# Turning the blocks of x behind the slabs, and who makes the low parts of slabs 1 and 3, at the start of a 1144-slab kernel

## What is computed

```
x = x + 0.5 * _swiglu(_rmsnorm(x, ffn1_norm[l]), ffn1_w_gu[l], ffn1_w_down[l])

def _rmsnorm(x, g):
    xf = x.astype(jnp.float32)
    y = xf * lax.rsqrt(jnp.mean(xf * xf, axis=-1, keepdims=True) + RMS_EPS)
    return (y * g.astype(jnp.float32)).astype(x.dtype)

def _swiglu(h, w_gu, w_down):
    gate, up = jnp.split(h @ w_gu, 2, axis=-1)
    return (jax.nn.silu(gate) * up) @ w_down
```

## Time and profile before

| | before |
|---|---|
| median of 3 runs | 3111.97 us |
| profiled execution | 3111.83 us, its span 3110.0 us |
| TensorE busy | 3072.0 us, 99% of the span |
| VectorE, ScalarE, GpSimd busy | 63%, 47%, 41% |
| DMA engines, mean | 212 GB/s read |
| granted TensorE clock, mean | 0.997 |

### The profile page before, as it was taken

How to read it: one execution, slowest core, us unless ns; L and a number is a source line. 1 busy time by engine, 2 the same in 40 slices (tenths; PEclk the granted TensorE clock), 3 DMA queues, 4 the chain that set the end, 5 groups by cost and what they waited for, 6 DMA issues and landing times.

```text
span 3110.0 us, 46519 instructions
## 1 busy us (share of the span) xinstructions
PE 3072.0 (99%) x19062; PEld 2714.9 (87%) x19062; DVE 1945.6 (63%) x2394; ACT 1446.4 (47%) x1877; POOL 1279.5 (41%) x621
## 2 busy tenths in 40 slices
PE   8999999999999999999999999999999999999998
PEld 7888888888999999998888888888899998899986
DVE  5777577773323446773466767676479864589764
ACT  5444444344567545544544444344444454444444
POOL 4444444444566554584444444444710004510013
PEclk9999999999999999999999999999999999999999
DMA  7878778785776555565787778787776545765454
GB/s 224 287 247 278 263 263 273 250 284 175 220 172 183 156 166 147 149 173 194 237 270 256 274 254 274 245 290 244 188 197 194 159 136 197 165 196 180 152 164 167
DMA packets 491774, 664.11 MB, mean 214 GB/s; under 512 B 74137, under 2 KB 278665, under 8 KB 491305
## 3 DMA queue, kind: packets, MB, share of 16 engines
q1 hardware_dynamic: 486072, 655.72, 67.1%
q0 software_dynamic: 4448, 3.64, 0.5%
q10 hardware_dynamic: 1040, 1.78, 0.2%
HBM read 656.82 MB, written 2.10 MB: 212 GB/s over the span
## 4 chain that ended last, share of the span: by engine, by line
PE 95%; DMA 1%; DVE 1%; ACT 1%; issue 1%; POOL 0%; SPq 0%; ACTq 0%; DVEq 0%
PE ps L891 36%; PE ps L819 22%; PE ps L896 18%; PE ps L825 11%; PE ps L809 2%; DMA stage<-in_w_in 1%; PE ps L850 1%; PE ps L1352 1%; PE ps L1137 1%; PE ps L1118 1%; POOL narrow_split_slabs L769 0%; PE ps L950 0%; PE ps L1045 0%; DMA x_res<-in_x 0%; PE ps L1175 0%
## 5 line engine op out<-in xcount | busy, mean ns | idle before, releaser
L769 POOL TENSOR_TENSOR split_slabs<-stage,split_slabs 128x1024 fp32r<-128x1024 f32 x296 | 751.0, 2538 | 1363.6 <-ACT split_slabs L1407 1363.6
L1407 ACT ACTIVATE split_slabs<-stage 128x1024 fp32r<-128x1024 f32 x592 | 627.1, 1061 | 903.9 <-PE ps L896 675.0
L891 PE MATMUL ps<-split_slabs,h_split 128*128 128x512 f32 x3312 | 827.1, 392 | 0.9 <-ACT split_slabs L1407 0.9
L1407 ACT ACTIVATE narrow_split_slabs<-stage 128x1024 fp32r<-128x1024 f32 (+1 forms) x440 | 460.3, 1051 | 651.7 <-PE ps L825 543.5
L819 PE MATMUL ps<-h_split,narrow_split_slabs 128*128 128x256 f32 x5856 | 746.9, 280 | 0.0
L891 PEld LDWEIGHTS ps<-split_slabs,h_split 128*128 128x128 f32 x3312 | 621.0, 188 | 133.3 <-issue 5.1
L819 PEld LDWEIGHTS ps<-h_split,narrow_split_slabs 128*128 128x128 f32 x5856 | 701.4, 188 | 15.8 <-issue 13.0
L1826 DVE TENSOR_TENSOR split_slabs<-stage,split_slabs 128x1024 fp32r<-128x1024 f32 x296 | 408.3, 1382 | 364.8 <-ACT split_slabs L1407 364.6
L769 POOL TENSOR_TENSOR narrow_split_slabs<-stage,narrow_split_slabs 128x1024 fp32r<-128x1024 f32 (+1 forms) x181 | 435.5, 2415 | 316.7 <-ACT narrow_split_slabs L1407 308.9
L896 PE MATMUL ps<-split_slabs,h_split 128*128 128x512 f32 x1656 | 443.2, 389 | 0.3 <-POOL split_slabs L769 0.3
L1826 DVE TENSOR_TENSOR narrow_split_slabs<-stage,narrow_split_slabs 128x1024 fp32r<-128x1024 f32 x259 | 330.0, 1276 | 176.0 <-ACT narrow_split_slabs L1407 174.4
(11 more groups left out here) (248 smaller groups left out, 2136.5 us busy)
## 6 DMA issues: line engine op xcount, KB each, us to landing
stage<-in_w_in SPq DMA_DIRECT2D x360, 512.0 KB, 3.7
stage<-in_ffn_w_gu SPq DMA_DIRECT2D x352, 512.0 KB, 4.9
U<-in_w_ada SPq DMA_DIRECT2D x192, 512.0 KB, 5.7
stage<-in_ffn_w_down SPq DMA_DIRECT2D x176, 512.0 KB, 5.4
stage<-in_w_out SPq DMA_DIRECT2D x96, 512.0 KB, 4.2
stage<-in_w_in SPq DMA_DIRECT2D x80, 128.0 KB, 2.8
stage<-in_w_branch_c SPq DMA_DIRECT2D x32, 192.0 KB, 3.4
stage<-in_cmp_w SPq DMA_DIRECT2D x8, 512.0 KB, 5.7
```

What stands on the lines that cost most here:

```text
L769: nc.gpsimd.tensor_tensor(slab_part(n, 1, size(n)), stage[:, n % RING, 0:size(n)], slab_part(n, 0, size(n)).bitcast(F32), ALU.subtract).th ...
L891: mm(ps[:, 2 * pair + T, :], stationary(kk, i)[:, T * P:(T + 1) * P], w[0][:, kk, :], start=first and kk == 0 and i == 0, stop=False)
L1407: return fn(slab_part(n, 0, size(n)), stage[:, n % RING, 0:size(n)], ACT.Copy)
```

## The change

Four things are done differently, all at the start.

1. TensorE turns only block 0 before slab 0. Blocks 1, 2, 3 are turned behind slabs 0, 1, 2; before, blocks 2 and 3 were turned behind slabs 0 and 1.
2. ScalarE rounds slab 1 before block 1, not behind it.
3. `by_vector` gets slabs 1 and 3 of the first layer, so GpSimd leaves them out.
4. VectorE makes the low part of slab 1 behind `rest_h` of block 1, and that of slab 3 ahead of `rest_h` of block 3. The loads of slabs 5 and 7 now wait for VectorE's signal.

```
-        by_vector |= {S_F2 + 1, S_F2 + 3}
+        by_vector |= {S_F1 + 1, S_F1 + 3, S_F2 + 1, S_F2 + 3}
...
-                            if (f, j, side) == (0, 0, 0) and q in (0, 1):
-                                turn_first(2 + q)
+                            if (f, j, side) == (0, 0, 0) and q < 3:
+                                turn_first(1 + q)
...
             turn_first(0)
             pe.wait_ge(gain_in, 16)
             turn_params(0)
-            turn_first(1)
             ffn(0, S_F1, G_F1, 0)
...
             for b in range(4):
-                if b > 1:
+                if b > 0:
                     round_upto(S_F1 + b)
                 round_h(0, b, pcol("ffn1_norm", 0, DC))
...
                 def between(i):
-                    if f == 0 or i not in (1, 3):
+                    if i not in (1, 3):
                         slab_lo(s0 + i)
...
             for b in range(4):
+                if b == 3:
+                    slab_lo(S_F1 + 3)
                 rest_h(0, b, pcol("ffn1_norm", 0, DC))
+                if b == 1:
+                    slab_lo(S_F1 + 1)
```

## The result

The changed kernel takes 3118.41 us, the median of 20 runs (3114.22 to 3125.32); the kernel before took 3112.76 in 20 runs made beside them (3105.74 to 3118.12). The ratio is 1.0021 with a 95% interval from 1.0015 to 1.0027, so it is slower by 4.7 to 8.4 us (the two medians lie 5.65 apart). The size at which a difference counts, 6.2 us, lies inside that interval. The profiled execution took 3119.17 us with a span of 3117.4.

What follows compares the result with a forecast made beforehand. TensorE, busy 99% of the span, was taken as the bound; an earlier slab 0, less new waits and moved work, gave +4.7 us: 3116.7 us (+0.15%), main account 3115.5 to 3118.0, wide range 3114.0 to 3121.5.

Steps and rivals of the forecast that it cites:

- Steps 1 and 2: Slab 0 on TensorE starts at 11.3 us (-1.6), runs at the slow rate (+0.6) and ends at 16.4.
- Step 3: TensorE turns block 1 behind slab 0, taking 1.1 us and ending at 17.5 us.
- Step 4: In the middle of slab 1 TensorE waits 1.95 us for VectorE's low part, ready at 21.3 us.
- Step 5: Block 3's transposes on TensorE end at 26.7 us instead of 22.02, +4.7 us in sum.
- Step 6: ScalarE's 11.7 us chain carries block 3's lateness on: TensorE waits 3.6 us in slabs 4 to 6; slab 6 starts at 38.5.
- Step 7: The rest costs nothing: from slab 6 on all moves by the same amount, and nothing gives the 4.7 us back.
- rival B: TensorE's clock falls in slab 1's 1.95 us pause, adding 3.5 us, for 3120.2 us; chance 0.04.
- Rival A: GpSimd starts slab 2's low part before VectorE starts slab 1's: 3119.0 us, or 3122.5 if the clock falls; chance 0.20.

Runs made afterwards that it cites:

- e3: Changed kernel, but VectorE makes slab 1's low part ahead of block 1's instructions instead of behind them; ratio 1.0012.
- e2: Kernel before, with only the low parts of slabs 1 and 3 moved to VectorE; ratio 0.9997.
- e1: Changed kernel, but the low parts of slabs 1 and 3 made by GpSimd again; ratio 1.0013.
- e4: Changed kernel, but ScalarE's second two blocks of squares stand behind slab 7 instead of slab 5; ratio 1.0026.
- e7: Changed kernel, but VectorE makes slab 1's low part twice, first into an unread scratch tile; one run, slab 8 starts at 49.56 us.
- e8: Changed kernel with ScalarE's order of before, rounding block 1 ahead of slab 1; ratio 1.0021.
- e5: Changed kernel with slab 1's low part ahead of block 1, second two blocks of squares behind slab 7, and five small loads spread behind slabs 9 to 13's loads; ratio 1.0000.
- e6: Kernel before, with only ScalarE's second two blocks of squares moved behind slab 7; ratio 0.9991, and 0.9992 when repeated.

## Why the prediction was right, and where not

The time lay in the wide range, 1.7 us above the point I gave (0.8 of these are the kernel before, 3112.76 in 20 runs for 3111.97 in three) and 0.4 above the narrow range of the main account, 3115.5 to 3118.0. The sign of the small loss and its place were as forecast. Step by step:

- *Steps 1 and 2, slab 0.* It started at 11.47, not 11.3, since x itself landed 0.2 us later in that execution. Its end, 16.59, was 0.2 later than said. The length was right, 5.13 us for 5.12, but by luck: the high pass took 3.78 and not 3.41, since it stands behind a wait here, and the low pass 1.35 and not 1.71, since the fast rate came earlier than in the trace before. The 5.8 us from which I took it were one draw.
- *Step 3, block 1.* It took 0.89 instead of 1.1, and ended at 17.48 (17.5 said). Right, with two misses of 0.2 us that cancel.
- *Step 4, the new wait.* Low part ready at about 21.2 (21.3 said), pause 1.91 us (1.95 said). e3 shows that its place in VectorE's queue makes it, e2 that the engine does not. What I left out is the refilling: a low pass behind a wait takes 1.19 us, not 0.92.
- *Step 5, block 3.* It ended at 26.93, +4.9 (26.7 and +4.7 said).
- *Step 6, ScalarE's chain carries it on.* Slab 6 started at 38.71 (38.5 said). The pauses of slabs 4 to 6 were 0.32, 0.32 and 2.19 us, and slow restarts make up the rest of the 3.6. e1 and e3 have the same 2.2 us ahead of slab 6 behind an earlier block 3, and e4 removes it by shortening the chain.
- *Step 7, "the rest costs nothing", and rival B.* This is the term that was wrong. I gave 0.04 to a fall of the clock behind a pause of 1.95 us, and leaned on the earlier trace rows, where a pause of 3.44 us had left it at 1.00. That row was one draw. The same pause of 3.44 us in the changed kernel's trace was followed by the slow rate:

```profile
2224.68 3.50 PE L809 MATMUL ps<-base_consts,U 128*128 128x128 f32 x16 [3.44 <-DVE U L1787]
```

3.50 us for sixteen transposes where the earlier trace rows has 1.97. In the 14 traces of this study that pause was always 3.44 us, and the transposes behind it took 2.38 to 3.68 in all but one: the 1.97 of the earlier trace rows, on which I leaned, is the exception. So whether a pause of 2 to 3.5 us costs the clock differs between executions of one program. Behind the pause of 1.9 us it fell in three of four traces, so 0.04 was far too low. I also had the price wrong, in the other direction, and it is luck that the two errors left the time near the point: 3.5 us for a whole slow s1, block 2 and high pass of s2, where the fall was over within them and cost 1.0 at slab 6 (5.94 - 4.92) and 1.6 behind slab 1 (slab 2's high pass 2.86 instead of 1.84, the turning of block 2 1.46 instead of 0.87).
- *Rival A* did not come about: VectorE led by 0.15 us, as worked out. e7 shows the turn-taking itself.

Of the profiled execution's +7.4 us of span, 5.9 are at slab 8, and the difference is still 5.96 us at 860 us, so the prediction's "nothing gives the 4.7 back" and "moved as a block" hold that far. Behind it the two traces drift: the transposes of the earlier trace rows start 4.87 us later than before (2224.68 for 2219.81), those behind the next long pause 7.44 us later (2667.20 for 2659.76). 1.5 of that are the slower transposes at 2224, which have nothing to do with the change; what gave 1.1 us back between 860 and 2220 is not traced to its cause.

That the time came out at 1.0021 and not at 1.0015 is then these parts: waits, restarts and order +4.9 us, the clock +1.0 to 1.6 in an execution, together 5.9 to 6.5 against 6.5 measured with an interval of 1.9 us to each side. The three traced marks, 45.89 to 46.31, give 5.8 to 6.2. So the sum fits the measurement, but an interval this wide would also fit a sum 1 or 2 us off; what carries the account are the waits and starts in the traces.

Left open: how often the clock falls behind each pause. It fell behind 3 of 4 pauses of 1.9 us and behind 1 of 7 of 2.2 us, which is too few to give a share.

## What to carry to other kernels

Moving work from a stretch in which the full engine waits for data anyway to one in which it does not gains only the start, and gives it back as soon as the moved work stands in the way of another engine's chain. Ask of each step moved back who hangs on its result: here a 0.9 us transposition released a chain of 11.7 us on ScalarE, and its 4.9 us of lateness went through in full although TensorE had done other useful work meanwhile. A helper's product belongs in its queue where its inputs are ready, not behind something that the waiting engine must do first. And one trace of a pause is one draw of what the clock does behind it.

## What the runs showed of the hardware beyond that

- TensorE's granted clock fell once in the first 60 us of each of the three traces of the changed kernel, behind 2.2 us in one and 1.9 in two, and in e4 (1.9) and e8 (2.6); the lowest stretch of 4 us showed 0.58, 0.77, 0.68, 0.76 and 0.60. It held at 1.00 behind 1.9 us in the first trace and behind 2.2 in e1, e3, e7, e8 and both repeats. Behind 5.2 us in e7 it was 0.50. The Trainium skill, page "TensorE: Matmul & The Clock Gate", section "HAM oscillation — how this bites in real kernels", warns of idle gaps of TensorE that let the clock fall; the traces agree that a gap does it, but here gaps of 1.9 us sometimes did.
- A gap is not needed. In six of the 14 traces the clock also fell once near 880 us, within 1.5 us behind twenty transposes, sixteen of them of 30 x 30 only, with no pause of TensorE just ahead; the other eight traces kept 1.00 there. In e5 (the stretch's 0.58 is the clock; the 16 matmuls of the last row took 2.15 in the kernel before):

```profile
876.00:880.00 4.00, 4.00 (x24) 4.00 (x23) 1.01 (x1) 0.06 (x1) 0.00 (x0) 0.58 1.08 229
```

```profile
873.25 2.20 PE L1080 MATMUL ps<-base_consts,U 30*128 30x30 f32 x16
875.38 2.76 PE L821 MATMUL ps<-h_split,narrow_split_slabs 128*128 128x256 f32 x16
```

- Five broadcast loads of 4 KB on SyncE's queue hold up a load of 512 KB issued right behind them: 9.2, 9.2 and 9.4 us to landing in e4, e6 and its repeat, against 3.8 and 3.9 where 3.5 us lay between, and 4.2 with one small load ahead of it. In e6 again the DMA engines were busy for 5% of four of these microseconds.
- Low parts made by VectorE and GpSimd at one time are made in turns: in the earlier trace rows, in the changed kernel (GpSimd's of slab 2 took 3.31 us for 2.4, VectorE having started 0.15 us ahead) and in e7 the one that comes second takes its own time plus what is left of the other's, less 0.1 to 0.2 us.
